# Mixture-of-experts stage on one core: finishing output rows inside the tile loop instead of in a pass behind it

## The reference, cut to what matters

```python
h2 = modulate(rmsnorm(x, norm2_g), sh2, sc2)
# router: the best of 4 groups, in it the best 2 of 4 experts, gates w2
a, b = h2 @ w_gate[e], h2 @ w_up[e]                   # 1024 -> 256, 16 experts
out  = sum over the token's 2 experts of (silu(a) * b * gate) @ w_down[e]
x = x + g2 * out
y = rmsnorm(x, final_norm_g)                           # the output rows
```

## Time and profile before

| | us |
|---|---|
| three runs: median (lowest to highest) | 1169.64 (1169.25 to 1170.22) |
| the profiled execution, its own time | 1168.66 |
| its span in the trace | 1166.9 |
| scatter of tile 39, the loop's last one, starts at | 1104.82 |
| last matmul of the last `down` starts at | 1126.79 |

### The profile page before, as it was taken

The page is one execution under the profiler, slowest core; times in us unless marked ns, Lnnn a source line. Parts: engine busy times, 40 slices in busy tenths (PEclk is TensorE's granted clock), DMA queues, the critical chain, the costliest instruction groups (busy, mean ns, idle before and its releaser), DMA issues. The chain is left out here.

```text
span 1166.9 us, 18010 instructions
## 1 busy us (share of the span) xinstructions
PE 1075.8 (92%) x5413; PEld 807.6 (69%) x5414; DVE 776.5 (67%) x1274; ACT 509.0 (44%) x715; POOL 308.4 (26%) x359
## 2 busy tenths in 40 slices
PE   3799999999969989999999989999999999999992
PEld 2357777776546667777787646888888788888860
DVE  4557475747789973369887778555777555555375
ACT  5133242522132325446665344555565445455273
POOL 0046262625041000030000003333333433333344
PEclk9799999999889999999999999999999999999997
DMA  9933646467776449485766566797789777775597
GB/s 280 316 108 101 193 137 193 150 180 226 200 190 164 136 160 242 167 234 201 252 218 222 176 221 229 244 292 221 220 257 291 216 216 216 218 216 110 111 358 310
DMA packets 166412, 244.75 MB, mean 210 GB/s; under 512 B 65783, under 2 KB 123271, under 8 KB 162207
## 3 DMA queue, kind: packets, MB, share of 16 engines
q1 hardware_dynamic: 138001, 171.05, 45.8%
q0 software_dynamic: 16112, 54.88, 18.0%
q10 hardware_dynamic: 12246, 18.14, 4.6%
HBM read 169.36 MB, written 75.84 MB: 210 GB/s over the span
## 5 line engine op out<-in xcount | busy, mean ns | idle before, releaser
L126 PE MATMUL experts_psGU<-weights_we_hi,experts_x_hi 128*128 (+1 forms) x344 | 140.6, 409 | 2.0 <-DVE experts_x_lo L2667 1.0
L127 PE MATMUL experts_psGU<-weights_we_hi,experts_x_lo 128*128 (+1 forms) x344 | 136.1, 395 | 0.0
L128 PE MATMUL experts_psGU<-weights_we_lo,experts_x_hi 128*128 (+1 forms) x344 | 136.0, 395 | 0.0
L2493 POOL DMA_INDIRECT acc_d<-experts_o_sb,experts_to_col x40 | 71.2, 1779 | 209.1 <-DMA acc_d<-experts_o_sb,experts_to_col 99.9
L126 PE MATMUL front_psM<-front_hT_hi,front_w_hi 128*128 128x512 f32 x256 | 106.7, 417 | 0.9 <-DVE front_hT_lo L1005 0.7
L2686 DVE TENSOR_TENSOR experts_o_sb<-experts_psD,experts_g2r 128x1024 f32<-128x1024 f32 x43 | 52.7, 1225 | 74.5 <-PE experts_psD L128 74.5
L127 PE MATMUL front_psM<-front_hT_hi,front_w_lo 128*128 128x512 f32 x256 | 101.6, 397 | 0.0
L128 PE MATMUL front_psM<-front_hT_lo,front_w_hi 128*128 128x512 f32 x256 | 101.2, 395 | 0.0
L126 PEld LDWEIGHTS experts_psGU<-weights_we_hi,experts_x_hi 128*128 128x128 f32 x344 | 64.7, 188 | 19.9 <-issue 5.2
L128 PEld LDWEIGHTS experts_psGU<-weights_we_lo,experts_x_hi 128*128 128x128 f32 x344 | 64.7, 188 | 15.6
L2657 DVE TENSOR_TENSOR weights_we_lo<-weights_we_raw,weights_we_hi (+1 forms) x64 | 75.4, 1219 | 0.0
(11 more groups left out here) (521 smaller groups left out, 2521.0 us busy)
## 6 DMA issues: line engine op xcount, KB each, us to landing
front_raw<-in_w_ada SPq DMA_DIRECT2D x24, 1024.0 KB, 7.8
weights_we_raw<-in_exp_w_gate SPq DMA_DIRECT2D x16, 1024.0 KB
weights_we_raw<-in_exp_w_up SPq DMA_DIRECT2D x16, 1024.0 KB
weights_wd_raw<-in_exp_w_down SPq DMA_DIRECT2D x16, 1024.0 KB
front_xraw<-in_x_prompt SPq DMA_DIRECT2D x4, 2048.0 KB, 10.9
part_d<-middle_ev ACTq DMA_DIRECT2D x16, 512.0 KB, 3.0
middle_xt<-in_x_prompt SPq DMA_DIRECT2D x16, 512.0 KB, 4.9
middle_part<-part_d SPq DMA_DIRECT2D x16, 512.0 KB, 5.5
```

The lines of the kernel that those rows point to most:

```text
L126: pe.matmul(out, l_hi, r_hi, start=start, stop=False)
L127: pe.matmul(out, l_lo, r_hi, start=False, stop=False)
L128: return pe.matmul(out, l_hi, r_lo, start=False, stop=stop)
L2493: pool.indirect_dma_start(acc_d, bass.IndirectOffsetOnAxis(tc[:, u, :], 0), osb[:, u, :], None, compute_op=ALU.add).then_inc(added, 16)
```

## The change

1. Routing marks which of a token's two slots is the later one (sign of the gate, `R.last`), and makes for each tile four index columns, `R.rows`: the token to gather; the row to add to, out of bounds for a later slot; the row to read back, out of bounds for an earlier slot; the row of y to store to, out of bounds for an earlier slot.
2. In the loop GpSimd's `scatter` becomes `sums`: the adding scatter, and right behind it a gather that adds the rows of `acc_d` onto `osb[u]` for later slots. Out-of-bounds rows are dropped by the DMA. So a later slot's row is x + both contributions.
3. Three tiles' worth of delay later the rows are finished: ScalarE `row_squares(s-3)` (square, sum), GpSimd `power(s-3)` (plus eps, to the power -0.5), VectorE `row_norm(s-3)` (a correction step in three small operations, then row times factor times `gn` into `fo[u]`), GpSimd `store(s-3)` (indirect DMA to y).
4. `g2r` has one buffer: `gate_rows(t)` waits for `out(t-1)`. The scheme with the pass over all rows, its loads, flags and stores is gone.
5. Behind the loop: late rows are summed by VectorE (`late_sums`) and GpSimd, TensorE only does the products with M and S.

The core of the diff:

```diff
-            def scatter(t, u):
-                pool.tensor_copy(tc[:, u, :], R.to[:, bass.ds(t, 1)]).then_inc(tc_ok, 1)
-                pool.wait_ge(tc_ok, t + 1)
+            def sums(t, u):
                 pool.wait_ge(oev, OEV0 + t + 1)
...
                     pool.wait_ge(added, 16 * t)
                     pool.sem_inc(freed, 1)
...
-                pool.indirect_dma_start(acc_d, bass.IndirectOffsetOnAxis(tc[:, u, :], 0), osb[:, u, :], None,
-                                        compute_op=ALU.add).then_inc(added, 16)
+                pool.indirect_dma_start(acc_d, bass.IndirectOffsetOnAxis(W.cols[:, u, 1:2], 0), osb[:, u, :], None,
+                                        bounds_check=TOK - 1, oob_is_err=False, compute_op=ALU.add).then_inc(added, 16)
+                pool.indirect_dma_start(osb[:, u, :], None, acc_d, bass.IndirectOffsetOnAxis(W.cols[:, u, 2:3], 0),
+                                        bounds_check=TP - 1, oob_is_err=False, compute_op=ALU.add).then_inc(acc_in[u], 16)
+            def power(t, u):
+                pool.wait_ge(fsq, FSQ0 + t + 3)
+                pool.tensor_scalar(fss[:, u, 1:2], fss[:, u, 0:1], EPS, None, ALU.add).then_inc(powers, 1)
+                pool.wait_ge(powers, 2 * t + 5)
+                pool.tensor_tensor(fss[:, u, 2:3], fss[:, u, 1:2], half[:], ALU.pow).then_inc(powers, 1)
+            def store(t, u, to):
+                pool.wait_ge(normed, NORM0 + t + 3)
+                pool.indirect_dma_start(y_p, bass.IndirectOffsetOnAxis(to, 0), fo[:, u, :], None,
+                                        bounds_check=TP - 1, oob_is_err=False).then_inc(y_out[u], 16)
...
             with pool.Fori(6, last + 1, 2) as t:
                 for d in range(2):
                     pool.wait_ge(xt_ps, t + d - 1)
+                    pool.wait_ge(acc_in[d], 8 * (t + d - 6) - 8 * d + 16 + ACC0)
+                    pool.wait_ge(y_out[d], 8 * (t + d - 6) - 8 * d + YOUT0)
                     W.gather(pool, R, h2_d, t + d, d)
-                    scatter(t + d - 4, d)
+                    power(t + d - 6, d)
+                    sums(t + d - 4, d)
+                    store(t + d - 6, d, W.cols[:, d, 3:4])
...
+            def row_squares(t, u):            # ScalarE
+                act.wait_ge(acc_in[u], 8 * t - 8 * u + 16 + ACC0)
+                act.activation(junk[:], osb[:, u, :], ACT.Square, scale=1.0 / 32, accum_out=fss[:, u, 0:1]).then_inc(fsq, 1)
...
                     x_hi_of(s + 1, 1 - u)
+                    row_squares(s - 3, 1 - u)
                     silu(s, u)
...
+            def row_norm(t, u):               # VectorE
+                v, y0, w, h, y = [fss[:, u, j:j + 1] for j in range(1, 6)]
+                dve.wait_ge(powers, 2 * t + 6)
...
+                dve.scalar_tensor_tensor(out=fo[:, u, :], in0=osb[:, u, :], scalar=y, in1=F.gn[:],
+                                         op0=ALU.mult, op1=ALU.mult).then_inc(normed, 1)
...
                     hidden(s, u)
+                    row_norm(s - 3, 1 - u)
                     out(s - 1, 1 - u)
...
+            power(end - 2, 0)                 # GpSimd behind the loop, after the three late gathers
+            store(end - 2, 0, last_to[:, 0, :])
...
+            def late_sums(n, ps, done):       # VectorE; n = 2: fix + osb3, the samples' two sums, fix + psC
```

More of the change, by code:

```diff
@@ L2499, in expert_pool @@
                 if t >= 4:
-                    scatter(t - 4, t % 2)
+                    power(t - 6, t % 2)
+                    sums(t - 4, t % 2)
             with pool.Fori(6, last + 1, 2) as t:
@@ L2584, in squares @@
+            def squares(n):
+                if n == LATE_A:
+                    act.wait_ge(fsq, FSQ0 + end + 2)
+                if n < LATE_C:
+                    act.wait_ge(own_sum, n + 1)
+                elif n == LATE_C:
+                    act.wait_ge(c_sum, 1)
                 else:
                     act.wait_ge(s_x3, 1)
-                for r, x in enumerate(unit(n)):
-                    if r not in blocks:
-                        continue
-                    if n != ORDER[0] or r:
-                        act.wait_ge(sq, SQ[n] - len(unit(n)) + r)
-                    act.activation(junk[0:x.shape[0], :], x, ACT.Square, accum_out=part(n, 0)[:, r:r + 1]).then_inc(sq, 1)
+                if n:
+                    act.wait_ge(sq, n)
+                x = unit(n)
+                act.activation(junk[0:x.shape[0], :], x, ACT.Square, accum_out=part(n, 0)).then_inc(sq, 1)
@@ L2636, in expert_act @@
             hidden_hi(end + 1)
-            squares(ORDER[0], (0,))
+            row_squares(end - 1, 1)
             silu(end + 2, 0)
-            gate_rows(end + 1, 1)
-            squares(ORDER[0], (1,))
+            gate_rows(end + 1)
             act.wait_ge(eps_ok, 1)
-            root(ORDER[0])
             hidden_hi(end + 2)
-            gate_rows(end + 2, 0)
-            for n in ORDER[1:]:
+            gate_rows(end + 2)
+            for n in ORDER:
                 squares(n)
@@ new lines, in norm @@
+                dve.scalar_tensor_tensor(out=x, in0=x, scalar=part(n, 2), in1=F.gn[0:x.shape[0], :],
+                                         op0=ALU.mult, op1=ALU.mult).then_inc(late_done if n < SAMPLES else s_done, 1)
+            def late_sums(n, ps, done):
+                dve.wait_ge(late_in[n], 16)
+                if n == 2:
+                    ch.link(dve.tensor_tensor(fix[:, n, :], fix[:, n, :], osb3[:], ALU.add))
+                    dve.wait_ge(s_in, 48)
+                    ch.link(dve.tensor_tensor(xs[:], xs[:], g2s[:], ALU.mult))
+                    ch.link(dve.tensor_tensor(xs[:], xs[:], x2[:], ALU.add))
+                dve.wait_ge(late_mm, n)
+                dve.tensor_tensor(fix[:, n, :], fix[:, n, :], ps, ALU.add).then_inc(done, 1)
@@ L2786, in expert_dve @@
             hidden(end + 1, 1)
+            row_norm(end - 2, 0)
             out(end, 0)
-            late_parts()
             with dve.If((code & 1) > 0):
@@ L2794, in expert_dve @@
             hidden_lo(end + 1)
-            late_flags()
             hidden(end + 2, 0)
+            row_norm(end - 1, 1)
             kept_rows()
@@ L2799, in expert_dve @@
             hidden_lo(end + 2)
-            store_rows()
-            norm(0)
-            norm(1)
+            late_sums(1, psB, b_sum)
             out(end + 2, 0, osb3[:])
-            for n in ORDER[2:]:
-                if n == LATE_C:
+            dve.wait_ge(oev, OEV0 + end + 3)
+            late_sums(2, psC, c_sum)
+            for n in ORDER:
+                if n == SAMPLES:
                     sample_sum()
```

304 lines of the change are left out of this document (151 added, 153 removed).

## The result

| | kernel before | changed kernel |
|---|---|---|
| median, us | 1169.93 (1169.25 to 1170.32, 4 runs) | 1317.1 (1312.83 to 1321.53, 4 runs) |
| ratio to before | | 1.1252, 95% interval 1.1223 to 1.1281 |
| span of the profiled execution, us | 1166.9 | 1311.0 |
| from scatter of tile 0 to scatter of tile 39, us a tile | 9.54 (372.2 in all) | 13.48 (525.8 in all) |
| from the start of the last scatter to the end, us | 62.1 | 47.4 |

The change made the kernel 12.5% slower. The prediction had the sign and the mechanism, and was 81 us too low, outside its range.

A forecast was written before the change was run, and what follows sets the result against it. It took TensorE as the loop's bound before, at 9.5 us a tile, and transfers behind it; after, a GpSimd-VectorE ring of 11.55 us. +83.8 to out(39) and -17.7 behind gave +66.1: 1236 us, range 1197 to 1275.

The forecast's parts named there:

- The ring: In the loop: one lap, out to out, runs serially through GpSimd's list and VectorE's end, 11.55 us against TensorE's 9.5.
- The lap's small terms: In the loop's lap: power 0.56, three small steps 0.60, normalization 1.20, scatter start 1.03, store 0.98, within 11.55 us.
- the scatter's price for the read-back: In the loop's lap: the adding gather was taken to cost 1.61 us like the adding scatter, not 0.99.
- the hand-over to VectorE: In the loop's lap: passing from GpSimd's power to VectorE was estimated at 0.15 us.
- Contention: In the loop: issues held up by VectorE's weight subtractions add 7 us in all, with 0 and 14 as ends.
- The start: Before out(0): 0.9 us added, 0.4 for routing operations, 0.5 for the first row_norm; memset and index arithmetic cost nothing.
- Behind the loop: From the end of out(39) to the end: 45.4 us instead of 63.1, so -17.7.
- (1): Rival, in the loop: issues cost by rows kept, lap 9.45 us, TensorE stays the bound, 1152 us; chance 0.09.
- (2): Rival, in the loop: three issues cost partly by rows, lap 9.8 to 10.6, time 1165 to 1200 us; chance 0.10.
- Landings (3): Rival, in the loop: scatters landing after 12.5 us set the lap, queue shared with weight loads, 1263 us; chance 0.12.
- The clock (4): Rival, in the loop: TensorE's clock falls to 0.76 for its gaps, a tile takes 12.5 us, 1274 us; chance 0.05.
- if GpSimd's small operations or waits cost more than a copy's: Stated sign of being wrong, in the loop's lap: GpSimd's small operations were priced as a copy, 0.20 us each.

The follow-up runs named there:

- Two kernels that took the end of GpSimd's list out of it: Changed kernel with the reciprocal root on VectorE instead of GpSimd, 1189.06 us; changed kernel with GpSimd's power between read-back and store, 1188.93 us (one run).
- halves: Changed kernel with each subtraction that makes low halves of weights cut into two instructions: 1285.24 us, ratio 1.098.
- early gather: Changed kernel with power a tile early, third gather ahead of the index arithmetic, weights' low halves for 16 columns only from the third expert: 1151.14 us (one run).
- The runs without low halves: Changed kernel with weights' low halves for 16 columns only from the third expert, 1273.41 us; also with early power and early third gather, 1151.14 us (one run each).
- a second: Changed kernel with GpSimd's power ahead of the gather instead of behind it, same instructions: 1235.87 us (one run).
- a third: Changed kernel with GpSimd's power a tile early, right behind scatter and read-back, ahead of store and next gather: 1188.93 us (one run).

## Why the prediction was right in kind and wrong in size

The sum was +66.1; the spans differ by 1311.0 - 1166.9 = +144.1. The 78.0 between them, step by step (3 us more are that the profiled run was the fastest of its four):

- **The ring** is what I said it was: a lap from `out` to `out` through GpSimd's whole list and the end of VectorE's, TensorE waiting ahead of `down`, VectorE ahead of its first small operation, no wait for a landing. Two kernels that took the end of GpSimd's list out of it gave back 128 us each.
- **The lap's small terms: 11.55 predicted, 12.47 measured, 36 us over 39 laps.** Scatter 1.64 for 1.61, read-back 1.63 for 1.61, gather 1.00 for 0.99 were right; the choice of the scatter's price for the read-back, on which 24 us hung, held. What failed are the terms for small operations and hand-overs: the power with its gaps 0.96 for 0.56 (a power alone is 0.57, a copy 0.20), the three small steps 0.74 for 0.60, normalization to `out` 1.41 for 1.20, the scatter's start behind `out` 1.14 for 1.03, the store 1.04 for 0.98. Only the hand-over to VectorE was shorter, 0.04 for 0.15. In the 1.41, 1.29 are the operation and the rest is `out` starting behind it; I had taken an overlap of 0.08 from a row in which two operations without such a wait follow each other.
- **Contention: 7 predicted, 42 on the scatters.** This is the step that failed. I saw the stall in the earlier trace rows, and then took its sum over the kernel before as its price, with 14 as the end. They didn't meet more often: in the kernel before, too, 28 of 40 scatters began while a subtraction ran. But 20 of these began 1.1 us or more into one of 1.2 us and took 1.6 us; only 8 were held up. In the ring every scatter starts 1.14 us behind `out`, and the second subtraction behind `out` starts 1.0 to 1.1 us behind it, so the scatter begins 0.09 us into it and waits for nearly all of it: 27 times, 1.0 or 2.1 us each. (One began 0.02 us into it and wasn't held up.) With the two laps without a store (2.6), from `out` 735.51 to `out` 1261.24, the laps give 525.7 instead of 454.9, 70.8 more: 36 from the small terms, and 35 from this (525.7 - 39 x 12.47 = 39.4 measured, 7 - 2.6 = 4.4 predicted). Either miss alone would have moved the forecast to 1271 or 1272, inside the range of 1197 to 1275. The range's upper end had room for 31 us of small operations, where 36 came, and for 14 of contention, where 42 came: it is contention that carried the time out of it.
- **The start: 0.9 predicted, 5.0 measured** (`out(0)` at 735.51, before at 730.54). I had called the memset and the index arithmetic free, with a tile's time as cover. They are not (timelines of GpSimd and TensorE):

```profile
708.78 1.80 POOL L2481 MEMSET experts_o_sb<- 128x2048 f32 x1 [1.39 <-DVE all_sample L2314]
...
713.68 2.40 POOL L2497 TENSOR_SCALAR all_rows<-all_far 128x48 int32<-128x48 int32 x2
716.24 0.19 POOL L2024 COPY weights_idx_cols<-all_rows 128x4 int32<-128x4 int32 x1 [0.16 <-PE experts_psX L2871]
717.24 2.43 POOL L2027 DMA_INDIRECT weights_xg<-h_d,weights_idx_cols  x1 [0.81 <-POOL weights_idx_cols L2024]
...
726.92 1.42 PE L2871 MATMUL experts_psX<-all_ident,weights_xg 128*128 128x128 f32 x8 [2.78 <-DMA weights_xg<-h_d,weights_idx_cols]
```

  Before, this gather was issued at 711.82 in 0.96 us. It now comes 5.4 us later, and beside a subtraction, which adds 1.5. TensorE waits 2.78 us for it, and behind the wait its granted clock is 0.50 (1.2 GHz) from 728.0 to 730.6. With the wait gone (halves, or early gather) `out(0)` still comes 1.6 to 2.8 us later than before, counted from the first gather, and stands behind the first normalization, which waits 0.9 us for its power; that wait was in the prediction.
- **Behind the loop: -17.7 predicted, -14.6 measured** (48.5 us behind `out(39)`, before 63.1). Counted from the end of `out(39)` at 1262.47, `out(40)` ended at 14.5 (15.0 predicted), `out(41)` at 24.2 (23.2), `out(42)` at 30.6 (27.5), the last sum of late rows at 35.6 (32.4) and the samples' normalization at 45.2 (42.4). So the steps are the right ones, and the 3 us are lost between `out(40)` and `out(42)`. The timeline of TensorE shows two places. `down(41)` begins at 1280.93 after 7.56 us of idle time, at a granted clock of 0.50 (1.2 GHz), its matmuls taking 0.63 us instead of 0.39, until 1283.6. And `down(42)` begins at 1288.43, 1.7 us behind the end of `out(41)`, for the products with M stand ahead of it in TensorE's list (1.88 us for four); I had let it begin at once.
- **Rivals.** The ring doesn't close (1) and the issues aren't priced by kept rows (2): where no subtraction runs beside them, each of the four kinds costs the same to 0.05 us from its smallest to its largest. Landings (3) never set the lap, and its premise was wrong: the indirect DMAs don't share a queue with the weight loads. The profile's table of queues has them apart, `software_dynamic` (54.88 MB before, which fits its 101 indirect DMAs of about 0.5 MB) beside `hardware_dynamic` (171.05 MB). The clock (4) fell to 0.93 only and the ring hid it. The sign that I was wrong "if GpSimd's small operations or waits cost more than a copy's" came true: the power takes 0.57 us, a copy 0.20.

On contention I went by the row and against the Trainium skill's page "SBUF — State Buffer" (Who interferes with whom), by which a tensor_tensor was not seen to stall the writing of descriptors. The runs without low halves settle that: the same scatters take 1.64 us without and 2.63 to 3.71 us with a tensor_tensor begun 0.09 us before them. The same section also says that a VectorE instruction with two inputs in SBUF contends with a GpSimd instruction that reads SBUF. The subtractions have both inputs there, an indirect DMA has its indices there, and the stalls fit that sentence; that it's the indices is not shown, for no run here took them away.

## What to carry to other kernels

When work is spread over engines that look idle, write down each engine's list in order and follow it once around: if engine A's last step of a lap feeds B's step that feeds A's first, the lap is the sum of both, whatever their busy shares say; and the cheapest cure is to move the small step that is waited for (here two operations of 0.8 us) ahead of the issues in A's list, or a lap early. A stall between two engines is priced by how far into the other's instruction each issue begins, not by how often they meet: the old kernel's scatters mostly began at a subtraction's end, the ring's at its start, and a ring repeats the one place in every lap. By the same token a gain from cutting instructions into pieces may be a moved start and go away with the next change. And split a change before judging it: here the late sums alone cost 7 us behind the loop, and the whole change costs 12.5% in one order of GpSimd's list, 5.6% in a second and 1.6% in a third (the last two from one run each, to the mean of the kernel before).

## What was not expected of the hardware

- A subtraction of VectorE with both inputs in SBUF delays the issue of an indirect DMA that adds and that starts behind it until it has nearly ended: a scatter takes 1.64 us alone, 2.63 when it starts 0.09 us into one of 1.22, 3.71 into one of 2.28, 2.17 when it starts 0.03 us into one of 0.68, and 1.6 again when it starts 1.1 us into one of 1.22. Started at most 0.022 us behind it, it isn't delayed at all in any of the traces (1.60 to 1.67), whatever the size, and the subtraction takes 0.05 us more.
- A power of a 128x1 column takes GpSimd 0.57 us, over twice the addition beside it (0.24).
- Issuing an indirect DMA that adds costs 1.6 us of GpSimd's time in either direction, one that doesn't 1.0; the number of its rows that are out of bounds made no difference seen here.
